# GLA state updates begin at round 3 of the fifth tile's top-k, with the indexer heads and the waits behind them re-dealt

## The reference, cut to what matters

```
s = relu(einsum('bqhd,bsd->bqhs', qi, ki) * 32 ** -0.5)      # 4 heads, dim 32
score = einsum('bqhs,bqh->bqs', s, wi * 4 ** -0.5)
score = where(key_pos <= query_pos, score, -inf)
_, idx = lax.top_k(score, 256)
```

```
o_intra = where(tril, qe @ ke.T, 0) @ v
U = kd.T @ v
S_next = decay * S + U          # scanned over the 16 chunks
o = rmsnorm(o_intra + qe @ S) * silu(gate)
```

## Time and profile before

| | us |
|---|---|
| median of 3 runs | 3226.95 |
| lowest, highest | 3218.61, 3236.28 |
| profiled execution, device time | 3224.9 |
| its span | 3223.1 |
| TensorE busy | 2927.1 (91%) |
| VectorE busy | 1326.9 (41%) |
| ScalarE busy | 903.2 (28%) |
| GpSimd busy | 1033.6 (32%) |

### The profile page before, as it was taken

The page is one execution under the profiler, slowest core; times in us unless marked ns, Lnnn a source line. Parts: engine busy times, 40 slices in busy tenths (PEclk is TensorE's granted clock), DMA queues, the critical chain, the costliest instruction groups (busy, mean ns, idle before and its releaser), DMA issues.

```text
span 3223.1 us, 39797 instructions
## 1 busy us (share of the span) xinstructions
PE 2927.1 (91%) x16484; PEld 2229.9 (69%) x16484; DVE 1326.9 (41%) x2447; ACT 903.2 (28%) x1689; POOL 1033.6 (32%) x447
## 2 busy tenths in 40 slices
PE   6979887879899998898899899999999999997998
PEld 4746674557666666665688677777777777775786
DVE  7999986555544444444634301111111111113322
ACT  4322313352233333333311322222222222223112
POOL 2613371124221212122353233342232323242541
PEclk8979899989999999999899999999999999998999
DMA  4100021031111111111122111111111111113211
GB/s 98 33 20 27 20 62 51 9 105 41 47 40 46 46 40 40 46 40 44 59 68 72 48 44 40 40 40 40 40 45 34 46 40 40 40 40 125 59 46 59
DMA packets 222223, 154.96 MB, mean 48 GB/s; under 512 B 26278, under 2 KB 208972, under 8 KB 221916
## 3 DMA queue, kind: packets, MB, share of 16 engines
q1 hardware_dynamic: 206908, 107.34, 11.9%
q10 hardware_dynamic: 15136, 45.08, 3.8%
HBM read 132.93 MB, written 19.47 MB: 47 GB/s over the span
## 4 chain that ended last, share of the span: by engine, by line
PE 77%; DVE 13%; ACT 5%; issue 3%; POOL 1%; DMA 1%; ACTq 0%; DVEq 0%; POOLq 0%
PE proj L820 20%; PE proj L821 19%; PE proj L822 19%; ACT arena L1723 3%; PE score L1106 2%; PE score L1092 2%; DVE arena L2154 2%; DVE arena L2152 2%; DVE arena L2206 2%; PE out L1121 2%; PE score L1235 1%; PE out L1288 1%; DVE arena L2289 1%; DVE arena L2211 1%; PE score L1244 1%
## 5 line engine op out<-in xcount | busy, mean ns | idle before, releaser
L820 PE MATMUL proj<-act_hi,w_hi 128*128 128x512 f32 x2592 | 1052.8, 406 | 46.7 <-POOL w_lo L695 28.3
L821 PE MATMUL proj<-act_lo,w_hi 128*128 128x512 f32 x2592 | 1025.4, 396 | 0.0
L822 PE MATMUL proj<-act_hi,w_lo 128*128 128x512 f32 x2592 | 1024.3, 395 | 0.0
L693 POOL TENSOR_TENSOR w_hi<-w_raw,ones 128x1024 fp32r<-128x1024 f32 x181 | 432.3, 2388 | 1844.2 <-PE proj L822 1827.3
L820 PEld LDWEIGHTS proj<-act_hi,w_hi 128*128 128x128 f32 x2592 | 496.8, 192 | 177.0 <-issue 33.6
L822 PEld LDWEIGHTS proj<-act_hi,w_lo 128*128 128x128 f32 x2592 | 496.2, 191 | 107.9
L821 PEld LDWEIGHTS proj<-act_lo,w_hi 128*128 128x128 f32 x2592 | 497.6, 192 | 99.6 <-issue 0.2
L695 POOL TENSOR_TENSOR w_lo<-w_raw,w_hi 128x1024 fp32r<-128x1024 f32 x181 | 448.9, 2480 | 14.2
L1707 ACT ACTIVATE arena<-proj 128x512 f32<-128x512 f32 x236 | 175.3, 752 | 922.5 <-PE proj L822 898.9
L2342 DVE SCALAR_TENSOR_TENSOR arena<-out,arena 128x128 f32<-128x128 f32 x64 | 17.9, 288 | 610.4 <-PE out L1254 610.4
L2188 DVE SCALAR_TENSOR_TENSOR arena<-score,arena 128x512 f32<-128x512 f32 (+2 forms) x192 | 109.6, 613 | 344.7 <-PE score L1092 344.7
(11 more groups left out here) (244 smaller groups left out, 3058.1 us busy)
## 6 DMA issues: line engine op xcount, KB each, us to landing
w_raw<-dil_w_in_dram SPq DMA_DIRECT2D x80, 512.0 KB, 3.7
w_raw<-fox_w_in_dram SPq DMA_DIRECT2D x32, 512.0 KB, 4.0
w_raw<-w_in_dram SPq DMA_DIRECT2D x23, 512.0 KB, 3.8
y_scratch<-arena ACTq DMA_DIRECT2D x21, 512.0 KB, 3.7
act_lo<-y_scratch ACTq DMA_DIRECT2D x21, 512.0 KB, 8.1
arena<-decay_scratch ACTq DMA_DIRECT2D x16, 512.0 KB, 5.3
w_raw<-ple_w_gate_dram SPq DMA_DIRECT2D x16, 512.0 KB, 3.8
arena<-x_dram SPq DMA_DIRECT2D x12, 512.0 KB, 4.1
```

What stands on the lines that cost most here:

```text
L693: pool.tensor_tensor(hi, raw, one.unsqueeze(1).broadcast_to([P, KB, P]), ALU.mult).then_inc(w_hi_done, 1)
L820: pe.matmul(bank, hi, a_hi, start=first, stop=False)
L821: pe.matmul(bank, hi, a_lo, start=False, stop=False)
L822: return pe.matmul(bank, lo, a_hi, start=False, stop=last)
```

## The change

The change moves work in the queues and adds or removes none.

```
-IDX_STEPS = {0: (5, 1), 1: (5, 2), 2: (5, 3), 4: (6, 0), 5: (6, 1), 6: (6, 2), 7: (6, 3),
-             12: (7, 0), 13: (7, 1), 14: (7, 2), 15: (7, 3)}
-GLA_ROUNDS = {4: range(12, 32, 3), 5: range(0, 32, 2), 6: range(0, 18, 2)}
-TURNED_AT = {(6, 30): 0, (6, 31): 1, (7, 3): 2, (7, 5): 3, (7, 7): 4, (7, 9): 5}
+IDX_STEPS = {0: (5, 1), 1: (5, 2), 2: (5, 3), 6: (6, 0), 7: (6, 1), 8: (6, 2), 9: (6, 3),
+             14: (7, 0, 1), 15: (7, 2, 3)}
+GLA_ROUNDS = {4: range(3, 32, 3), 5: range(0, 32, 2), 6: range(0, 12, 2)}
+TURNED_AT = {(6, 24): 0, (6, 25): 1, (6, 28): 2, (6, 31): 3, (7, 2): 4, (7, 4): 5}
...
             between = {...
-                       14: (lambda: heads(6, 0), lambda: heads(6, 2)), 17: (...),
+                       15: (lambda: heads(6, 0), lambda: heads(6, 2)), 17: (...),
...
                 pieces = {...
-                          (6, 20): inverse_roots, (7, 17): lambda: pool_outputs(0), (7, 26): lambda: pool_outputs(1)}
+                          (6, 14): inverse_roots, (7, 12): lambda: pool_outputs(0), (7, 21): lambda: pool_outputs(1)}
```

More of the change, by code:

```diff
@@ L785, in _ @@
                        9: (decayed_keys, lambda: heads(4, 2)), 11: (lambda: heads(5, 0), lambda: heads(5, 2)),
-                       14: (lambda: heads(6, 0), lambda: heads(6, 2)), 17: (lambda: heads(7, 0), lambda: heads(7, 2)),
+                       15: (lambda: heads(6, 0), lambda: heads(6, 2)), 17: (lambda: heads(7, 0), lambda: heads(7, 2)),
                        18: (lambda: gates((0, 1, 2)),), 19: (lambda: gates((3, 4)),), 21: (first_windows,),
```

## The result

| | before | changed |
|---|---|---|
| median of 20 runs, us | 3228.71 | 3241.69 |
| lowest, highest, us | 3218.61, 3240.63 | 3232.27, 3255.62 |
| profiled execution, span | 3223.1 | 3253.8 |

The ratio is 1.0044, 95% interval 1.0031 to 1.0057: the change costs about 14 us. The forecast was 3.5 us slower, no difference that can be measured, with a range that ended at 3241. It was wrong: the loss is clear of zero and four times the forecast.

The account below looks back on a forecast made before the run. TensorE bounds the kernel nearly everywhere, but VectorE's queue bounds this stage. Terms 0 + 0 + 3.1 + 0.4 = +3.5 us on the profiled 3224.9 gave 3228.4, carried to a median of 3230; range 3218 to 3241.

Parts of the forecast that it names:

- chain: Work from the reciprocals to the second pooling output, taken as rigid: 109.8 us, wherever the reciprocals stand.
- The output waits: VectorE's waits for gated and pooling outputs (L1029 and L1039): 7 to 8 us, against 8.6 before.
- TensorE's last wait: TensorE idle ahead of the first attention pair: some 22 us where it was 9.2, counted as free.
- Term: 0: Updates from round 3, in tile 4: no VectorE waits expected there, 0 us, bounds 0 and 6.
- I take 4.5 after: Tile 6's heads in steps 6 to 9, in tile 5: VectorE waits 4.5 us as before, bounds 0 and 8.
- a cold step at 6 us: Tile 4: one GLA step at TensorE's lower clock would cost 6 us, the upper bound; 0 was taken.
- the pair steps, +4.1: Tile 7's heads two a step in steps 14 and 15: tile 6 waits 6.4 us for 2.3, bounds -2.3 and +13.
- Rival B: Pair steps 14 and 15 stay at 1.2 GHz: +9 to +10 us on top of +3.5, 3240; chance 0.12.
- VectorE's own work stays the same: VectorE keeps 192 rounds, 32 updates and 10 outputs; only its 15.4 us of waits can move the end.
- a forecast of +0.4: First attention pair, met cold by TensorE after a longer idle: +0.4 us, bounds 0 and +4.
- That is 0.5% of the time and the most that can be won: VectorE's 15.4 us of waits in the stage, as the limit on any gain.
- 0.89 to no change: Chance that the whole kernel's time measures the same; faster had 0.04, slower 0.07.

Follow-up runs that it names:

- e6: The kernel before with the reciprocals 3 rounds earlier, one round behind the last update; 0.21% faster than before (0.05 to 0.36%).
- e7: The changed kernel with the reciprocals 3 rounds earlier, one round behind the last update; 337.0 us between the mask ends of tiles 3 and 7 (changed 347.7).
- e1: The changed kernel with tile 7's heads back at one a step, in steps 12 to 15; distance of the mask ends of tiles 3 and 7 fell by 3.3 us.
- e5: The changed kernel with 8, 4 and 8 extra unused matmuls in GLA steps 3, 4 and 5; time ratio 1.0034 to before.
- g3: Start at round 3, wider update spacing for head steps, one head a step, earlier reciprocals, later outputs, extra matmuls; 0.48% faster than before (0.34 to 0.61%).
- e3: The changed kernel with gated and pooling outputs back at the rounds of the kernel before; time back to that of before.
- e2: The changed kernel with tile 6's heads back at steps 4 to 7, their sum ahead of weight 14; mask ends of tiles 3 and 7 3.4 us further apart.
- e4: The changed kernel with all indexer heads back at the steps of the kernel before, keeping the earlier start; time 0.24% above before.

## Why the prediction was wrong

**Right: who sets the end, and how the end follows.** The stage ends with VectorE's queue. The start of the mask is still reciprocals, chain, and ten rounds: 374.38 + 111.6 + 1.6 + ten rounds of 2.58 = 513.3 us, the row above. No waits came in tile 4 either, as forecast. The chain took 111.6 where I had 109.8. That it came out near does not show it to be rigid: with the reciprocals moved by 6.9 us, the outputs' waits fell by only 3.2 and 5.3 us (e6, e7). The output waits were forecast at 7 to 8 us and were 8.9. TensorE's last wait was forecast at 22 us and was 22.1.

**Wrong: "Term: 0" for the earlier start, and "so they cost VectorE what they did" with "I take 4.5 after" for the steps of tile 5.** This is the step that failed. I looked for waits of VectorE in tile 4 only, and took equal spacing in tile 5 for equal cost. What the wide spacing of tile 4 does is let TensorE stand idle for 1.2 to 2.2 us a step. Behind the longer of those gaps the clock fell, the last time at the entry to tile 5, where the steps are tight and carry heads. Tile 5 had 9 to 11 us in three executions of four, +4.6 to +6.7 for a term of 0. e7 (same program up to there, no fall at the entry: 3.6) and e5 (gaps filled, falls gone: 6.3) point the same way; since e7 shows what one execution can do by chance, e5's waits alone would not prove it. The forecast had priced a cold step at 6 us, as a bound, and put it in the wrong tile. Its upper bound for tile 5, called twice the 4.5, was written as 8; twice is 9, and 11.3 lies beyond both.

**Mis-sized: the pair steps, +4.1.** The mechanism was right, and e1 bears it out (3.7 us with one head a step). Turn to turn I had 14.1 us and 1.6 for the clock, 15.7; it was 17.46. The second head, its wait of 1.12 us and the spacing were as computed; the fall took the logits, both products and most of the half pass, 3.4 us in place of 1.6. Step 15 waited 4.5 us for its logits and 1.3 for U, where I had 3.0. Tile 6: 8.6 to 10.8 for a forecast of 6.4, that is +6.3 to +8.5 for a term of +4.1. Rival B had this place and nearly the time, 3240 us. But it wanted the clock low through both steps and +9 to +10 us from them on top of the forecast; they gave +2 to +4 on top of their forecast, and tile 5, which B left out, gave +5 to +7 in the executions whose clock fell. The price was right partly by luck.

**Missed: the masks.** No term stood for L2159, whose three instances of tiles 4 to 6 went from 0.49 + 0.56 + 0.62 to 1.44 + 0.95 + 1.08 us, +1.8 (last section). The claim that VectorE's own work stays the same was off by this much.

**Added up.** Head waits 19.9 - 6.8 = 13.1, outputs +0.3, masks +1.8: 15.2 us by waits, 14.8 by D. The forecast had 4.1 - 1.0 = 3.1. Behind the stage the first pair's first 24 dense matmuls took 7.55 us for 6.51: +1.0 for a forecast of +0.4, and nearer to the milder end as said.

**"That is 0.5% of the time and the most that can be won"** was not contradicted: g3, the best here, won 0.48% (0.34 to 0.61%). But a bound on the gain bounds no loss. I gave 0.89 to no change on the strength of it, while the two things that could cost more were written down as bounds of 6 and 13 us.

Not settled: why the time of e3 is that of before while its D is 9.1 us above it, what makes tile 6 of e2 so bad, why the clock stayed up in tile 5 of e7, how the loss divides between start and heads, and what the chain hangs on when the reciprocals come earlier.

## What to carry to other kernels

Where two engines hand work to each other at a fixed spacing, compare the length of a step with the spacing at the lower clock of TensorE too, and above all just behind the places where a wide spacing lets it idle. An earlier start by itself is worth nothing when the other engine is the bound; what went with a gain of 0.5% here was to give steps with more work more room, to place each output where its input is ready, and to fill the idle gaps. When waits differ by several us between executions of one program, take a second profile before a term is sized.

## What the runs showed of the hardware that I had not expected

**A mask instruction that starts while a GpSimd tensor-tensor operation runs ends 0.3 to 0.5 us behind the end of that operation.** L2159 over 128x768 took 0.56 us before, with GpSimd idle, 2.17 in e1 and 2.58 in e2, with GpSimd busy. Timelines of POOL and DVE in e1, then in e2:

```profile
324.80 2.34 POOL L693 TENSOR_TENSOR w_hi<-w_raw,ones 128x1024 fp32r<-128x1024 f32 x1 [16.03 <-PE proj L822]
325.39 2.17 DVE L2159 TENSOR_SCALAR arena<-arena 128x768 bf16<-128x768 f32 x1
327.22 2.56 POOL L695 TENSOR_TENSOR w_lo<-w_raw,w_hi 128x1024 fp32r<-128x1024 f32 x1
...
322.13 2.39 POOL L695 TENSOR_TENSOR w_lo<-w_raw,w_hi 128x1024 fp32r<-128x1024 f32 x1
322.35 2.58 DVE L2159 TENSOR_SCALAR arena<-arena 128x768 bf16<-128x768 f32 x1
```

In e1 the mask ended at 327.56, 0.42 us behind the split that ended at 327.14; in e2 at 324.93, 0.41 behind the one that ended at 324.52. So the mask is not slowed by a factor: it waits for the operation in flight, and how long depends on where in it the mask falls. Over the masks of tiles 3 to 6 in all thirteen executions, 39 of 52 started inside such an operation and all 39 ended 0.27 to 0.49 us behind its end, the wider the later; the 13 others took 0.49, 0.56 or 0.62 us by width. A mask that started first was not held (0.56 us in e4, with a split starting 0.26 us behind it).

MAX8 and MATCH_REPLACE8 beside the same operations kept their lengths (0.96 and 0.94 us over 128x768, beside and alone). The Trainium skill ("VectorE: DVE Perf Modes", section "Two Vector instructions with no wait between them") speaks of a second SBUF read interface that is shared with GpSimd and is used by two-port modes; the durations fit that, and no run here separates it from other causes.

**TensorE's clock fell to 1.2 GHz behind gaps of 2.2 us, and behind heads without any gap.** In the kernels that start at round 3, twelve of thirteen gaps of 2.2 to 2.4 us in steps 3 and 5 were followed by a fall; seven gaps of 1.2 to 1.5 us in step 4 and one of 2.0 (e1) were not. Filling gaps with unused matmuls kept the granted clock at 0.98 to 1.00 from 212 to 244 us in e5. Whether a given gap is followed by a fall differed between executions of one program: in e7 it stayed at 1.00 at the entry to tile 5, behind a gap of 2.2 us. The gap of 22.1 us ahead of the first pair cost 1.0 us more than one of 9.2 us.
